# First unit of four layers computed on x times the norm's weights, with GpSimd making its low parts

## The reference

```
y = x * rsqrt(mean(x*x) + eps)          # root mean square norm over the channels of a token
h = (y * g) * (1 + scale) + shift       # scale and shift: columns of c @ ada_w, the same for all tokens
... = h @ in_w ...                      # the first products of the layer
x = x + gate_res * (y2 @ out_w)         # the end of the layer
```

## Time and profile before

| what | value |
|---|---|
| median of 3 runs | 985.44 us (983.79 to 986.64) |
| the profiled execution's own time | 985.16 us |
| its span, first to last instruction | 983.4 us |
| PE busy | 951.5 us, 97% |
| PE weight loads busy | 875.3 us, 89% |
| DVE busy | 713.7 us, 73% |
| ACT busy | 508.8 us, 52% |
| POOL busy | 40.9 us, 4% |
| DMA, mean | 223 GB/s |
| chain that ended last | PE 88%, DVE 7%, DMA 2%, issue 2%, ACT 1% |

### The profile page before, as it was taken

How to read it: one execution, slowest core, us unless ns; L and a number is a source line. 1 busy time by engine, 2 the same in 40 slices (tenths; PEclk the granted TensorE clock), 3 DMA queues, 4 the chain that set the end, 5 groups by cost and what they waited for, 6 DMA issues and landing times.

```text
span 983.4 us, 17238 instructions
## 1 busy us (share of the span) xinstructions
PE 951.5 (97%) x7025; PEld 875.3 (89%) x7025; DVE 713.7 (73%) x994; ACT 508.8 (52%) x745; POOL 40.9 (4%) x68
## 2 busy tenths in 40 slices
PE   6999999999999999999999999999999999999998
PEld 5799989989899889999778889889998978898987
DVE  4778877767957946675998988967888765555554
ACT  4654364446645555644755456475555554444444
POOL 2100000000000013210100000000000000000000
PEclk9999999999999999999999999999999999999999
DMA  9998676846875877576577887774534457676631
GB/s 365 385 342 257 211 268 231 283 129 226 291 259 167 295 261 250 179 260 213 155 254 255 281 274 263 246 257 136 172 119 138 131 172 247 184 223 212 192 101 43
DMA packets 134247, 219.43 MB, mean 223 GB/s; under 512 B 8585, under 2 KB 100090, under 8 KB 134168
## 3 DMA queue, kind: packets, MB, share of 16 engines
q1 hardware_dynamic: 132416, 214.99, 66.3%
q0 software_dynamic: 992, 1.76, 0.7%
q10 hardware_dynamic: 760, 1.59, 0.4%
HBM read 217.25 MB, written 1.05 MB: 222 GB/s over the span
## 4 chain that ended last, share of the span: by engine, by line
PE 88%; DVE 7%; DMA 2%; issue 2%; ACT 1%; ACTq 0%; DVEq 0%
PE pw L568 62%; PE pacc L568 24%; DVE WL L1659 1%; DMA ring<-in_ada_w 1%; DVE SQT L1755 1%; DVE hl L1760 1%; PE pw L1021 1%; DMA cst<-in_consts 1%; DVE ACC L1675 1%; ACT hh L1174 1%; DVE AR L1675 0%; PE pw L997 0%; DVE xT L2059 0%; ACT WH L1174 0%; ACT SQT L1174 0%
## 5 line engine op out<-in xcount | busy, mean ns | idle before, releaser
L1174 ACT ACTIVATE WH<-ring 128x1024 fp32r<-128x1024 f32 x288 | 302.7, 1057 | 271.1 <-PE pw L568 171.7
L1659 DVE TENSOR_TENSOR WL<-ring,WH 128x1024 fp32r<-128x1024 f32 x288 | 348.3, 1224 | 84.2 <-ACT WH L1174 83.5
L568 PE MATMUL pacc<-YH,WH 128*128 128x256 f32 x672 | 192.8, 287 | 2.7 <-issue 1.7
L568 PE MATMUL pacc<-YH,WL 128*128 128x256 f32 x672 | 190.1, 283 | 0.0
L568 PE MATMUL pacc<-YL,WH 128*128 128x256 f32 x672 | 190.0, 283 | 0.0
L568 PE MATMUL pw<-hh,WH 128*128 128x256 f32 x704 | 186.7, 287 | 1.5 <-DVE WL L1659 0.8
L568 PE MATMUL pw<-hh,WL 128*128 128x256 f32 x704 | 183.9, 283 | 0.0
L568 PE MATMUL pw<-WH,hh 128*128 128x512 f32 x448 | 177.3, 396 | 2.8 <-DVE WL L1659 2.3
L568 PE MATMUL pw<-WL,hh 128*128 128x512 f32 x448 | 175.2, 391 | 0.0
L568 PE MATMUL pw<-hl,WH 128*128 128x256 f32 x704 | 142.6, 284 | 0.0
L568 PEld LDWEIGHTS pw<-hh,WH 128*128 128x128 f32 x704 | 134.8, 191 | 6.0 <-issue 5.7
(11 more groups left out here) (272 smaller groups left out, 778.2 us busy)
## 6 DMA issues: line engine op xcount, KB each, us to landing
ring<-in_w_mod SPq DMA_DIRECT2D x72, 512.0 KB, 4.7
ring<-in_odd_in_w SPq DMA_DIRECT2D x56, 512.0 KB, 5.8
ring<-in_ada_w SPq DMA_DIRECT2D x48, 512.0 KB, 6.9
ring<-in_ffn_w_gate SPq DMA_DIRECT2D x88, 256.0 KB, 3.3
ring<-in_ffn_w_up SPq DMA_DIRECT2D x88, 256.0 KB, 4.3
ring<-in_ffn_w_down SPq DMA_DIRECT2D x44, 512.0 KB, 4.6
ring<-in_even_in_w SPq DMA_DIRECT2D x40, 512.0 KB, 6.5
ring<-in_even_out_w SPq DMA_DIRECT2D x16, 512.0 KB, 5.6
```

Source lines behind the costliest of these rows:

```text
L568: return eng.matmul(o, a, b, start=start, stop=stop, skip_group_check=True)
L1174: return eng.activation(dst, src, func, **kw)
L1659: tt(WL[:, i % NL, :], slot(half_of(i)), WH[:, i % NH, :].bitcast(F32), SUB).then_inc(s_lo, 1)
```

## The change

1. **The first unit of the odd layer, of both feed-forwards and of the mixer** no longer waits for the norm. For each tile k, ACT rounds x times `GS` into `hh` straight from `xT` (`early`); POOL computes the same product again into a buffer and subtracts `hh` to get `hl` (`lows`, two instructions for each tile). Two more columns of `hh`/`hl` hold the shift. PE's `first` multiplies 258 columns, with the shift's product in the last ones. The sums of squares stand in it in two parts (after the layer's last product: tiles 0 to 3; behind the first tile: tiles 4 to 7), the spread of the root behind the fourth tile. When it is done, ACT copies the result and the root from PSUM (`RAW`, `RB`), POOL multiplies them (`rooted`), and ACT adds the shift's product (`biased`, or inside the Silu of the feed-forwards).
2. **The modulated `hh`/`hl`** are still made by ACT and DVE, over the same buffers, after the first unit has read them, for all other units of the layer (`between` on DVE: update, low part of one piece, root, low part of the next piece, modulate).
3. The first block of the feed-forwards is two `cols_T` units of 256 columns; it needs no `turn`. `warm` between these layers is gone.
4. `RING` 9, `NH` 5, `AHEAD_H` 4 (`AHEAD_L` stays 2).
5. Ada steps are kept away from the last and the first units (`QUIET`, `lead`); the ada loads are a little denser elsewhere. Side jobs begin after the first two units of the first feed-forward.
6. Mixer order: `wc0` (the first unit), `wu0`, `wu1`, `s5_in(0)`, `wv0`, `s5_in(1)`, `wb0`, `s5_out(0)`, `wc1`, `s5_turn(0)`, `wv1`, `s5_out(1)`, `wb1`, `s5_turn(1)`, `glu`.
7. Odd layer: one gate unit (`og`) earlier, none behind the last `gr` pair; the low-rank products stand inside `qk1`; an ACT table is loaded earlier.

```diff
-RING = 10
-NH, NL = 4, 4
-AHEAD_H, AHEAD_L = 3, 2
+RING = 9
+NH, NL = 5, 4
+AHEAD_H, AHEAD_L = 4, 2
...
+            def first(L, z, c=0):
+                name = FIRST[L]
+                k, a = unit(name)
+                names = first_banks(L)
+                bks = [open_(nm, None, True) for nm in names]
+                for half in range(2):
+                    H, Lo = piece(2 * k + half, a)
+                    for kk in range(4):
+                        i = 4 * half + kk
+                        if i == 1:
+                            later[L - 1]()
+                            back(f"fin{L - 1}")
+                        if i == 4:
+                            spread(f"r{L}", c, z, (s_rb, L), True)
+                        p.wait_ge(s_eh, 8 * (L - 1) + i + 1)
+                        for m, pb in enumerate(bks):
+                            mm(pb[:, 0:T + 2], H[:, kk, m * P:m * P + P], hh[:, i, 0:T + 2], i == 0, False)
+                            mm(pb[:, 0:T + 2], Lo[:, kk, m * P:m * P + P], hh[:, i, 0:T + 2], False, False)
+                        p.wait_ge(s_el, 8 * (L - 1) + i + 1)
+                        for m, pb in enumerate(bks):
+                            last = mm(pb[:, 0:T + 2], H[:, kk, m * P:m * P + P], hl[:, i, 0:T + 2], False, i == 7)
+                    last.then_inc(s_use, 1)
...
+            def early(L, sh, c, scale=1.0):
...
+                for q in range(4):
+                    ns = (2 * q, 2 * q + 1)
+                    if q == 3:
+                        squares(L - 1, ns)
+                        cut_on(L - 1)
+                    for n in ns:
+                        s.wait_ge(s_x, X_FIN[L - 1] + n + 1)
+                        act(hh[:, n, 0:T], xT[:, n, :], scale=GS[:, n:n + 1]).then_inc(s_eh, 1)
+                    if q < 3:
+                        squares(L - 1, ns)
+                k = unit(FIRST[L])
+                cut(2 * k)
+                modulate(L, sh, range(4))
+                for m, nm in enumerate(first_banks(L)):
+                    s.wait_ge(*full[nm])
+                    act(RAW[L][:, m, :], pw[place[nm]][:, 0:T + 2], scale=scale).then_inc(s_bank[place[nm]], 1)
+                cut(2 * k + 1)
+                modulate(L, sh, range(4, 8))
+                act(RB[L], pw[place[f"r{L}"]][:, 0:T]).then_inc(s_rb, 1)
...
+            def between(L, g, sh, root):
+                update(L - 1, g)
+                k = unit(FIRST[L])
+                cut(2 * k)
+                root()
+                cut(2 * k + 1)
+                mods[0] += 1
+                modulate(L, sh, range(8))
...
+            def lows(L, sh):
...
+                for k in range(8):
+                    xg = XG[L][:, k % 2, :]
+                    g.wait_ge(s_x, X_FIN[L - 1] + k + 1)
+                    eng.tensor_scalar(xg, xT[:, k, :], GS[:, k:k + 1], None, MUL).then_inc(s_eg, 1)
+                    g.wait_ge(s_eh, 8 * (L - 1) + k + 1)
+                    g.wait_ge(s_eg, 8 * (L - 1) + k + 1)
+                    eng.tensor_tensor(hl[:, k, 0:T], xg, hh[:, k, 0:T].bitcast(F32), SUB).then_inc(s_el, 1)
+
+            def rooted(L, dsts):
+                g.wait_ge(s_rb, L)
+                for m, nm in enumerate(first_banks(L)):
+                    g.wait_ge(*gone[nm])
+                    eng.tensor_tensor(dsts[m], RAW[L][:, m, 0:T], RB[L], MUL).then_inc(s_em, 1)
```

More of the change, by code:

```diff
@@ L218, in ada_places @@
     m, unit = 0, None
+    names = [u[0] for u in units if u[0] != "ada"] + [None]
+    behind = dict(zip(names, names[1:]))
     for nm, *_ in units:
@@ L630, in cols_T @@
                                     (half == 0 and kk == 0, False), half == 1 and kk == 3)
+                        if behind is not None and (half, kk) != (1, 3):
+                            behind(4 * half + kk)
                     last.then_inc(s_use, 1)
@@ L715, in sums, with rest @@
                         stats(st["pb"][:, 0:256], w, k, SQ_FIN[L] + k, k == 0, k == 7)
+                def rest():
+                    sums(2)
+                    sums(3)
+                    full[f"fin{L}"] = (s_sqr, sqr_n[0])
+                later[L] = rest
                 def tail(q, h):
@@ L719, in tail @@
                         st["pb"] = open_(f"fin{L}", None, True)
-                    if weights is not None and q >= 2 and h == 0:
-                        sums(q - 2)
                     if q == 3 and h == 1:
[L723 to L728, removed]
-                return tail
[L731 to L737, removed]
+                        sums(0)
+                        sums(1)
+                        if L == L_F2:
+                            rest()
+                return tail
+            later = {}
+            def first(L, z, c=0):
[20 more added lines that the diff above has]
+                    last.then_inc(s_use, 1)
+                for nm in names:
+                    full[nm] = used(name)
+                    back(nm)
                 back(f"r{L}")
@@ L1038, in ffn @@
                                  finish(L) if blk == 11 else None, (lambda: turn(blk)) if blk < 11 else None)
[L1040 to L1053, removed]
+            side.rate = 0
             side.gens.append(s5_weights())
+            first(L_F1, 4, 10)
             ffn(L_F1, "f1", Y_F1)
             side.flush()
-            norm_mod(L_MIX, 5)
             def s5_in(h):
@@ L1101, in _ @@
             side.rate = 0
+            first(L_MIX, 5)
             for j in range(2):
@@ L1509, in s5_prep, with ffn @@
                     yield
-            def ffn(tag, y0, n0):
-                for blk in range(12):
+            def ffn(L, tag, y0, n0):
+                pieces(f"{tag}u0")
+                if tag == "f1":
+                    evac("xnew", XNW, src=pw[place["xnew"]][:, 0:T])
+                    side.rate = 1
+                for m in range(2):
+                    s.wait_ge(s_em, 2 * (L - 1) + m + 1)
+                    act(fbuf(0, m), fbuf(0, m), ACT.Silu, bias=RAW[L][:, m, T:T + 1]).then_inc(s_sl, 1)
+                for blk in range(1, 12):
                     if blk < 11:
@@ L1966, in _ @@
             gates = iter(range(8))
+            pieces(f"og{next(gates)}")
             v.wait_ge(s_kqe, 3)
@@ L2181, in ffn @@
             def ffn(tag, y0, n0):
-                for blk in range(12):
+                pieces(f"{tag}u0")
+                if tag == "f1":
+                    side.rate = 1
+                b = place[f"{tag}u0"]
+                for m in range(2):
+                    v.wait_ge(*full[f"{tag}u0"])
+                    v.wait_ge(s_sl, n0 + m + 1)
+                    a = tt(fbuf(0, m), fbuf(0, m), pw[b][:, m * T:m * T + T], MUL)
+                a.then_inc(s_bank[b], 1)
+                for blk in range(1, 12):
                     if blk < 11:
```

302 lines of the change are left out of this document (164 added, 138 removed).

## The result

The changed kernel takes 1002.51 us (median of 4, 1000.77 to 1004.35) against 985.50 us for the kernel before in the same comparison: ratio 1.0174, 95% interval 1.0151 to 1.0198. It is 17 us slower. The forecast was 982.0, the range 974 to 991.

What follows compares the result with a forecast made beforehand. PE is nearly always busy; four layer bounds hold at most about 16 us of gaps. Gains of 8.7 less 1.7 and 3.6 give 3.4 off 985.16, 981.8, or 982.0 with the median's 0.28; range 974 to 991.

Steps and rivals of the forecast that it cites:

- the slack: First unit at each changed bound: POOL has tile 7 ready at 786.1, PE asks at 787.1, 1 us spare.
- the first rival: At the four bounds GpSimd sets the pace, 1.5 us a tile instead of 1.1: 991 to 995, chance 0.22.
- the signs of being wrong: At the bounds: PE's waits for POOL's hl over 4 us, root instructions over more than 4 us, long wait before the spread.
- the new bound: Layer change, mixer to second feed-forward, redone step by step: third unit starts 16.7 us after the last product.
- The second feed-forward's bound: Mixer to second feed-forward: 1.7 us won, plus 0.44 for the dropped turn, 2.1 in all.
- The bound to the mixer: Entry to the mixer: 18.9 us before against 16.7, 2.2 won; late `urs` copies lose 1.7.
- The first feed-forward's bound: Entry to the first feed-forward: 3.7 us won, 1.5 taken back because DVE is full there, so 2.2.
- DVE's full stretch: First feed-forward, DVE busy 29.28 of 30 us, PE waiting 2.31 at its end: 1.5 us of gain taken back.
- The chain into `glu`: Mixer: `wb1` no longer covers the gelu, so second half of `glu` starts at 751.4 instead of 747.8; loses 3.6 us.
- the third rival: Gain given back by lower clock before `glu` (1 to 2), ring (1 to 2), DVE's full stretch: 986, chance 0.14.
- Ring: nothing (0 to 2): First layer's weight loads, needed one piece sooner with one slot fewer: counted as nothing, 0 to 2 us.
- The odd layer's bound: Entry to the odd layer up to the low-rank pair: 20.65 us before against 18.4, 2.2 won.

Runs made afterwards that it cites:

- e8: Changed kernel with GpSimd's scaling written with two inputs (the weight spread with stride 0) instead of a per-partition scalar; 991.42 us, ratio 1.0065.
- e1: Changed kernel with GpSimd's two low-part instructions a tile cut to 2 of 256 columns, semaphores kept; 983.47 us, ratio 0.998.
- e5: e4 with the mixer's second-half gelu pulled forward, the turned halves standing inside `wb1`; 987.52 us, ratio 1.0024.
- e2: Changed kernel with the old buffer split: ring of 10 slots, 4 high weight buffers, high parts 3 ahead; 1001.48 us, ratio 1.016.
- e3: Kernel before with `hh` and `hl` in rows of 272 columns instead of 256, `GRW` and `RR` in the arena; 986.64 us, ratio 1.0008.
- e6: e4 with `hh` and `hl` in rows of 320 columns instead of 272 and four high weight buffers; 993.09 us, ratio 1.0079.
- e7: Changed kernel with five small warming products ahead of tiles 1 to 7 of each first unit; 1014.42 us, ratio 1.0293.
- e4: Changed kernel with the first units' low parts made on DVE, one instruction a tile, four before and four behind the root; 989.89 us, ratio 1.0044.

## Why the prediction was wrong

**The step that failed is GpSimd's price.** The prediction took 0.40 for the scaling (between a mask's 0.27 for 128 columns and 0.635 for 512) and 0.64 for the subtraction, 1.1 us a tile. The trace has 0.92 and 0.74 undisturbed with 0.1 between, 1.8, and 1.9 as a mean over all. The subtraction was too cheap by 0.1. The scaling was more than twice too cheap: a mask works in place and has no scalar read from memory, and it was taken as the row for a one-input operation all the same. e8 shows that the form matters (0.61 with two inputs); what a scaling in place or with a constant would take, no run shows. The prediction had named 1.35 us a tile as the point where the sign turns. The mechanism around the price was right: put 1.8 into the forecast's own sum and the last tile comes 8 x 0.7 = 5.6 us late, 4.6 after the slack, 18.4 over four bounds, and e1 and after differ by 19.0. e1 (nothing of it: 983.5) and e8 (1.6 us: 991.4) lie on both sides, and e8 lies where the first rival put 1.5 us (991 to 995). That rival, with a chance of 0.22, was the right one; at 1.9 it went past its own figure and past the end of the range. The range ended at 991 although the text itself bounded a tile at 2.44 us. Of the signs of being wrong that it named, one came (waits for POOL's low parts of 11.8 us in sum, where 4 was the mark); the root took 2.6 us at most and the spread waited 0.4, so the other two did not.

**What held.** e1 is the new bound without GpSimd's work, and it takes 983.5 where the forecast was 982.0. The closeness is in part luck. The forecast had 0.8 us a bound in it for the root that GpSimd stretches, and e1 has no such stretch, so without it the forecast would be about 979. And the 2.4 us that e1 gains before the first changed bound are in no term. By stretches, as e1 minus before:
- The second feed-forward's bound was to gain 2.1, or 2.9 with an unstretched root; e1 gains 2.8. The bound to the mixer: 2.2 less 1.7 for `urs`, 1.3 without the stretch; e1 gains 2.9, and PE waits 0.4 there, not 1.7. The root was to be stretched by 0.8: in after 795.76 to 798.31 is 2.55 against 1.61, so 0.9.
- The first feed-forward's bound was to gain 2.2. The stretch in e1 gains 0.2, but the sums that stood between the last products before now stand in it; with the 2.4 of the row above it is 2.6. DVE's full stretch, for which 1.5 was taken back, holds one wait of 3.1 in e1; in exchange the one of 2.31 is gone.
- The chain into `glu` was to lose 3.6: 3.7 in after, and 5.3 in e1, of which 1.5 is the lower clock behind the wait. That is what the third rival had said of this place (1 to 2). The mechanism is as written; e5's stretch gets 1.7 of it back.
- "Ring: nothing (0 to 2)": 1.0 in e2.

**What was missed besides.** The odd layer's bound was to gain 2.2, and e1 loses 1.1 there: PE waits 2.5 and 0.5 us for DVE's ada steps and low part. There are no more steps than before (eight between the start of the bound and PE's sum of them in both), but they come later: the first 18.8 us behind that start instead of 12.8, the third 33.3 instead of 20.3. Item 5 of the change keeps them away from a layer's first units. The ring is not what delays them: e2, with 10 slots, has the same 2.5 us. The prediction put no price on item 5; that this placing is the cause is read from the times of the steps and was not run. And "the 258 columns cost nothing" priced the columns, not the rows of 272 that they need: 2.0 us in the second feed-forward and 1.6 in the first (e3).

**What the Trainium skill said of GpSimd** ("GPSIMD Engine Reference", "4.1 Engine selection") spoke against the change, and was right in sign. The estimate of 0.56 us, worked out from the 4497 ns that the same page of the Trainium skill gives in "3.1 Elementwise — side-by-side cycle accounting", was under the 0.74 measured. With the rule of the Trainium skill on two-input VectorE work against GpSimd reads ("SBUF — State Buffer", "Who interferes with whom") the trace after agrees: 1.74 us instead of 0.74 beside DVE's cut. With e8's form it is the root that pays, 5.7 us of waits.

**Open.** Why the single-scalar form is slower than the two-input one was not tried further. What the placing of the ada steps alone costs was not run; the 3.3 us of waits for them stand in all versions of the change.

## What to carry to other kernels

Price an operation that moves to another engine from a row with the same form on that engine: the same number of inputs, the same kind of scalar, the same types. If no row has it, let the range reach what the far row gives, and find the pace at which the sign turns. An engine that is 11% busy can set the pace of the stretches where each of its results is waited for; and a longer buffer that only a corner of the kernel needs can be paid wherever its tiles are read.

## What the runs showed of the hardware

- GpSimd, 128 x 256 f32: multiplying by a scalar of each partition takes 0.92 us, by the same value spread with stride 0 as a second input 0.61 us, the subtraction of two full inputs into fp32r 0.74 us, all undisturbed.
- POOL's subtraction beside DVE's cut of a weight took 1.74 us instead of 0.74; the root's nine small DVE instructions took 1.61 us alone and 2.4 to 3.75 beside POOL's work.
- Stationary tiles `hh` and `hl` in rows of 272 columns (1088 bytes) slow PE's 512-column products: 17.32 us for a block, 17.09 with rows of 256 (1024 bytes) and 17.08 with rows of 320 (1280 bytes). What tells the free lengths from the other, no run shows.
- Behind waits of 0.5 to 1 us, one on each of four tiles 1.8 to 1.95 us apart, the granted clock fell to a mean of 0.90 (682 to 700). With two small products ahead of each tile it was 1.00, and the time stayed 1002.8. Behind one wait of 2.27 us before `glu` the clock fell in the profiles of e1, e6 and e7 and stayed whole in after's and e4's.
